# Seven products for every second row-block pair, and column-pair totals carried through the PSUM banks by ScalarE

## The reference, cut to what matters

```python
h2 = rmsnorm(x, norm2_g[l])                                   # x: 256 x 2048
x  = x + jnp.square(jax.nn.relu(h2 @ w_up[l])) @ w_down[l]    # w_up 2048 x 8192, w_down 8192 x 2048
```

## Time and profile before

| | us |
|---|---|
| median of 3 runs (2057.11 to 2057.16) | 2057.12 |
| the profiled execution | 2057.14 |
| its span, first to last instruction | 2055.3 |
| TensorE busy | 2038.4 (99%) |
| VectorE busy | 1520.6 (74%) |
| ScalarE busy | 1058.5 (51%) |
| pair stage of the second turn, 594.69 to 678.95 | 84.26 |
| up stage after it, 678.95 to 768.70 | 89.75 |

### The profile page before, as it was taken

The page is one execution under the profiler, slowest core; times in us unless marked ns, Lnnn a source line. Parts: engine busy times, 40 slices in busy tenths (PEclk is TensorE's granted clock), DMA queues, the critical chain, the costliest instruction groups (busy, mean ns, idle before and its releaser), DMA issues.

```text
span 2055.3 us, 26947 instructions
## 1 busy us (share of the span) xinstructions
PE 2038.4 (99%) x10644; PEld 1709.3 (83%) x10644; DVE 1520.6 (74%) x1961; ACT 1058.5 (51%) x1382; POOL 192.1 (9%) x196
## 2 busy tenths in 40 slices
PE   9999999999999999999999999999999999999999
PEld 7887788887887887888888877888788878878887
DVE  7767566788779769867677775666986896797674
ACT  6557644454455445444455586444544554554442
POOL 5253100000000000001023531000000000000000
PEclk9999999999999999999999999999999999999999
DMA  9477866666657665766665689566576566666663
GB/s 300 134 227 187 221 199 181 186 193 205 186 174 216 194 189 181 213 187 192 184 176 145 211 203 232 183 180 188 183 213 188 180 212 191 185 193 206 185 194 123
DMA packets 182879, 396.67 MB, mean 193 GB/s; under 512 B 13674, under 2 KB 22352, under 8 KB 182752
## 3 DMA queue, kind: packets, MB, share of 16 engines
q1 hardware_dynamic: 178064, 379.52, 61.1%
q0 software_dynamic: 4512, 15.33, 4.1%
q10 hardware_dynamic: 176, 0.09, 0.0%
HBM read 377.95 MB, written 2.12 MB: 185 GB/s over the span
## 4 chain that ended last, share of the span: by engine, by line
PE 85%; DVE 13%; issue 1%; DMA 1%; ACT 0%; SPq 0%; ACTq 0%
PE psum L570 23%; PE psum L594 23%; PE psum L597 12%; PE psum L574 12%; DVE w_lo L1086 4%; PE psum L641 4%; DVE t_lo L1094 2%; PE psum L604 2%; PE psum L644 2%; PE psum L608 2%; PE psum L605 2%; PE psum L697 1%; DVE x L1145 1%; PE psum L769 1%; DVE t_raw L1084 1%
## 5 line engine op out<-in xcount | busy, mean ns | idle before, releaser
L891 ACT CAST w_hi<-raw_ring 128x1024 fp32r<-128x1024 f32 (+1 forms) x720 | 747.4, 1042 | 857.0 <-PE psum L597 361.7
L1086 DVE TENSOR_TENSOR w_lo<-raw_ring,w_hi 128x1024 fp32r<-128x1024 f32 (+1 forms) x692 | 846.2, 1228 | 403.2 <-ACT w_hi L891 400.9
L594 PE MATMUL psum<-xt,w_hi 128*128 128x512 f32 x2048 | 515.1, 393 | 0.9 <-issue 0.3
L594 PEld LDWEIGHTS psum<-xt,w_hi 128*128 128x128 f32 x2048 | 368.4, 189 | 69.7 <-DVE x L1145 3.0
L597 PEld LDWEIGHTS psum<-xt,w_lo 128*128 128x128 f32 x2048 | 279.4, 190 | 20.0
L597 PE MATMUL psum<-xt,w_lo 128*128 128x256 f32 x2048 | 285.6, 282 | 0.0
L570 PE MATMUL psum<-w_hi,xt 128*128 128x512 f32 (+1 forms) x1152 | 281.4, 386 | 0.0
L570 PEld LDWEIGHTS psum<-w_hi,xt 128*128 128x128 f32 x1152 | 202.5, 189 | 40.3 <-issue 2.7
L570 PE MATMUL psum<-w_hi,ht_hi 128*128 128x512 f32 x512 | 203.1, 397 | 0.0
L570 PE MATMUL psum<-w_hi,ht_lo 128*128 128x512 f32 x512 | 199.8, 390 | 0.0
L641 PE MATMUL psum<-w_hi,ht_lo 128*128 128x512 f32 x384 | 149.5, 389 | 0.0
(11 more groups left out here) (200 smaller groups left out, 2140.8 us busy)
## 6 DMA issues: line engine op xcount, KB each, us to landing
raw_ring<-in_w_up_dram SPq DMA_DIRECT2D x256, 512.0 KB, 4.0
raw_ring<-in_w_down_dram SPq DMA_DIRECT2D x256, 512.0 KB, 4.2
raw_ring<-in_w_in_dram SPq DMA_DIRECT2D x128, 512.0 KB, 4.7
raw_ring<-in_w_out_dram SPq DMA_DIRECT2D x64, 512.0 KB, 4.9
w_lo<-raw_ring POOLq DMA_DIRECT2D x28, 512.0 KB, 6.9
raw_ring<-in_w_in_dram SPq DMA_DIRECT2D x16, 256.0 KB, 2.8
x<-in_x_dram SPq DMA_DIRECT2D x8, 256.0 KB, 7.8
out_dram<-x SPq DMA_DIRECT2D x3, 512.0 KB, 3.3
```

The lines of the kernel that those rows point to most:

```text
L594: pe.matmul(bank[:, f, :], w_hi[:, w, j, f * P:(f + 1) * P], both, start=kt == 0, stop=False, skip_group_check=True)
L891: act.copy(w_hi[:, u % AHEAD, :, 0:cols], raw_ring[:, u % RAWS, :, 0:cols]).then_inc(hi_ready, 1)
L1086: dve.tensor_tensor(w_lo[:, u % AHEAD, :, 0:cols], raw_ring[:, u % RAWS, :, 0:cols], w_hi[:, u % AHEAD, :, 0:cols].bitcast(F32), ALU.subtr ...
```

## The change

`SEVEN` becomes (1, 3, 5, 7) for both column pairs: each second pair of row blocks, and the last one of a column pair too. That is eight of sixteen in a turn. Column pair d = 1 now begins with plain units.

The totals of d = 0 no longer are added up in SBUF by VectorE. ScalarE copies them out of the banks at the border (`take_totals`), and at the start of the next turn of the layer copies them back into banks 0 to 3 (`give_totals`), where the products of that turn are added to them.

The last seven-product pair of a column pair is done in another order: second unit first, then the first, then all matmuls with `t_hi`, then the three with `t_lo`. The quarter adds follow it through `pair_done`. `last_unit` is gone. A seven-product pair reports its second unit as done before its `t` products, and its end through a semaphore of its own, `sevens_done`.

```diff
-SEVEN = ((2, 4, 6), (0, 2, 4, 6))
+SEVEN = (1, 3, 5, 7)
...
-            def seven_products(pl, s, d, kp, a, b, outs):
+            def seven_products(pl, s, d, kp, a, b):
...
+                new = first and (d == 1 or pl.i == 0)
...
                 if first and d == 0:
                     pe.wait_ge(evicted[0], pl.evictions(18))
+                    if pl.i:
+                        pe.wait_ge(totals_in, pl.l * (LOOPS - 1) + pl.i)
                 if first and d == 1:
-                    pe.wait_ge(pair_out, outs - PAIR_OUTS + 1)
+                    pe.wait_ge(totals_out, pl.l * LOOPS + pl.i + 1)
...
+                if last:
+                    quarters()
+                    own()
+                else:
+                    own()
+                    quarters()
...
                 if seven is not None and seven[0] == 1:
+                    if pair_at(pl, u)[1:] == (1, 2 * SEVEN[0] + 1):
+                        take_totals(pl, pair_at(pl, u)[0])
                     act.wait_ge(t_raw_ready, seven[1] + 1)
+                    if seven[1]:
+                        act.wait_ge(sevens_done, seven[1])
                     act.copy(t_hi[:, :, :], t_raw[:, :, :]).then_inc(t_hi_ready, 1)
...
+            def take_totals(pl, turn):
+
+                act.wait_ge(sevens_done, pl.l * SEVENS + (2 * turn + 1) * len(SEVEN))
+                act.copy(totals[:, :, :], psum[:, 0:4, :]).then_inc(totals_out, 1)
+
+            def give_totals(pl):
+
+                act.wait_ge(evicted[0], pl.evictions(18))
+                act.wait_ge(totals_out, pl.l * LOOPS + pl.i)
+                act.copy(psum[:, 0:4, :], totals[:, :, :]).then_inc(totals_in, 1)
...
             def mlp(pl, s, part, buf, c, k, n):
...
+                if part == "pair" and c == 0 and k == 0 and pl.i:
+                    give_totals(pl)
                 if pl.l < DEPTH - 1 or s + AHEAD < UNITS:
                     split_hi(pl, s + AHEAD)
...
-                if part == "pair" and c == 0 and k == 2 * KPS - 3:
-                    dve.wait_ge(unit_done, pl.unit(s + 1 + AHEAD))
-                    take_totals(pl)
                 if part == "pair" and k == 2 * KPS - 2:
-                    take_quarters(pl, s + 1, c)
+                    take_quarters(pl, s, c)
```

More of the change, by code:

```diff
@@ L645, in pair_steps @@
                     mm.then_inc(unit_done, 1)
[L647 to L653, removed]
-            def seven_products(pl, s, d, kp, a, b, outs):
-                i, first = SUMMED.index(kp), kp == SEVEN[d][0]
+            def seven_products(pl, s, d, kp, a, b):
+                i, first, last = SEVEN.index(kp), kp == SEVEN[0], kp == KPS - 1
                 _, number = seven_at(pl, s)
+                new = first and (d == 1 or pl.i == 0)
                 if d == 0:
@@ L671, in s_tile @@
                     return [t[:, i, n, :] for t in (s_hi, s_lo)]
[L673 to L680, removed]
@@ L681, in seven_products, with own @@
-                freed(2)
-                three(quarter(0, 1), s_tile(3), w_tile(s + 1, 1), kp == 0)
-                pe.wait_ge(t_lo_ready, number + 1)
[L684 to L687, removed]
+                def own():
+                    pe.wait_ge(hi_ready, pl.unit(s + 1))
+                    three(psum[:, 0, :], h_tile(a, 0), w_tile(s, 0), new, lambda: unit_is_split(pl, s))
+                    three(psum[:, 1, :], s_tile(0), w_tile(s, 1), new).then_inc(unit_done, 2 if last else 1)
@@ new lines, in quarters @@
+                def quarters():
+                    pe.wait_ge(hi_ready, pl.unit(s + 2))
+                    mm = three(quarter(0, 0), h_tile(b, 0), w_tile(s + 1, 0), False, lambda: unit_is_split(pl, s + 1))
+                    if last:
+                        mm.then_inc(pair_done, 1)
+                    mm = three(quarter(0, 1), s_tile(3), w_tile(s + 1, 1), False)
+                    mm.then_inc(pair_done if last else unit_done, 1)
+                if last:
+                    quarters()
[3 more added lines that the diff above has]
+                    quarters()
@@ new lines, in seven_products @@
+                products = [(quarter(1, 0), h_tile(b, 1), 2, False), (psum[:, 2, :], s_tile(1), 1, new), (psum[:, 3, :], s_tile(2), 0, new)]
+                pe.wait_ge(t_hi_ready, number + 1)
+                for bank, (a_hi, a_lo), t, start in products:
+                    pe.matmul(bank, a_hi, t_hi[:, t, :], start=start, stop=False, skip_group_check=True)
+                    pe.matmul(bank, a_lo, t_hi[:, t, :], start=False, stop=False, skip_group_check=True)
+                pe.wait_ge(t_lo_ready, number + 1)
@@ L689, in warm @@
+                for n, (bank, (a_hi, a_lo), t, start) in enumerate(products):
+                    mm = pe.matmul(bank, a_hi, t_lo[:, t, :], start=False, stop=True, skip_group_check=True)
+                    if last and n == 0:
+                        mm.then_inc(pair_done, 1)
+                mm.then_inc(sevens_done, 1)
             def warm(n):
@@ L1127, in quarter_x @@
                 return x[:, r, (2 * d + h) * CW:(2 * d + h + 1) * CW]
[L1129 to L1134, removed]
             def take_quarters(pl, s, d):
-                done = pl.at(2 * LOOPS * 3, 3 * d, 6)
                 for n, (r, h) in enumerate([(1, 1), (0, 0), (0, 1), (1, 0)]):
-                    if n < 3:
-                        dve.wait_ge(pair_done, done + n + 1)
+                    if n == 0:
+                        dve.wait_ge(unit_done, pl.unit(s + AHEAD))
                     else:
-                        dve.wait_ge(unit_done, pl.unit(s + 1 + AHEAD))
+                        dve.wait_ge(pair_done, pl.at(LOOPS * 6, 3 * d + n, 6))
                     v = quarter_x(r, h, d)
```

43 lines of the change are left out of this document (21 added, 22 removed).

## The result

| | before | after |
|---|---|---|
| median, us (5 runs each) | 2057.11 (2056.70 to 2057.16) | 2064.91 (2064.50 to 2065.15) |
| ratio after / before, 95% interval | | 1.004 (1.0029 to 1.0051) |
| profiled execution / its span, us | 2057.14 / 2055.3 | 2065.15 / 2063.3 |

The account below looks back on a forecast made before the run. VectorE's gapless queue was taken to bound each pair stage's first half. Two first turns at -0.55 and four later ones at +2.5 add 8.9 to 2057.14: 2066.0 us, own range 2062 to 2070, widened to 2058.5 to 2071 for 8 in 10.

Parts of the forecast that it names:

- VectorE's queue without the copies: Pair stage's start to first quarter add: changes of -2.20, +1.20, -0.60 and +0.25 sum to -1.35, adds at 42.0 us.
- The border and the stage: Between column pairs: TensorE starts 2.6 us after the adds begin, then 39.5 us; pair stage 84.1 against 84.28, -0.15.
- The up stage: At the up stage's start TensorE's 0.4 us wait goes: -0.4 us in each turn.
- The copy back: Second and third turns: ScalarE's 1.91 us copy into banks delays unit 4's cast; VectorE stands 3.04 us, arriving whole at the border.
- TensorE's waits inside the half: Later turns, first half: 2.2 us for banks at unit 2, probably 1 us at units 6 and 7, not added.
- The clock: A granted clock below 1.00 after the new waits was named a sign of being wrong; the trace showed 1.00 everywhere.
- The sum: Whole run: first turns -0.55 twice, -1.1; other four +2.5 each, +10.0; 2057.14 + 8.9 = 2066.0 us.
- TensorE the bound: Pair stages: VectorE's queue has unseen slack, stages -2.8 twice and -0.8 four times, 2048.3 us; chance 0.09, including the busy-time rule.
- Copy back free: Start of later turns: the copy into the banks costs VectorE nothing, all six turns gain 0.55, 2053.8 us; chance 0.04.
- made good: Before the border: half the delay recovered by waits counted as busy time, 6 us less, 2060.0 us; chance 0.07.
- came on top: TensorE's late units 6 and 7 add 1.1 us four times, with the copy at its upper price: 2071.9 us; chance 0.08.
- The rule of the Trainium skill: Optimize the highest-occupancy engine, TensorE: 18 fewer matmuls, 4.1 us off, 2053.0 us; shares the 0.09 chance of faster.

Follow-up runs that it names:

- the two kernels without the stall: Changed kernel with the copy back moved behind the cast of unit 4, 2054.44 us; changed kernel with no copy back, VectorE adding totals behind its quarter adds, 2053.24 us.
- The first experiment: Changed kernel with one swap on ScalarE: the copy of the totals into the banks stands behind the cast of unit 4; 2054.44 us.
- the third: Changed kernel with three extra small sums on VectorE per pair stage: ahead of the border 2082.39 us, behind it 2064.97 us.
- the last two kernels: Three quarter adds moved earlier, upon the kernels with early first t_hi and t_lo: 2042.60 us with copy back behind the cast, 2042.30 us with VectorE's totals.

## Why the prediction held, step by step

- **VectorE's queue without the copies.** 42.0 us from the stage's start to the quarter adds; measured 41.96 in both first turns, 41.97 in the two kernels without the stall. The 1.35 taken off is 1.35. The two kernels with three more sums show the premise at work: 2.20 us later ahead of the border, nothing behind it.
- **The border and the stage.** 84.1 was forecast, 84.07 and 84.08 measured. A wait of 1.4 us at the border remained, 0.8 in three of the later turns, where "1 us or more" was forecast. ScalarE's copy out started 42.3 us into a first turn and not at 41.3, and stayed hidden.
- **The up stage** lost 0.37 or 0.38 for 0.4 forecast (89.38). Its VectorE adds end at 681.54 for a start at 681.11.
- **The copy back.** Its duration was taken as 1.91 and is 1.87. It starts 5.64 us into the stage (5.66 forecast); VectorE stands 2.91 (3.04). Shown as the cause by the kernel that only changes the order of copy and cast: 10.5 us off between the profiled executions, four times 3.0 less the 1.5 of the slow stage. The later turns take 87.09 for 87.2.
- **TensorE's waits inside the half.** 2.14 for 2.2 at the banks. At units 6 and 7, 1 us was forecast and 0.64 came, in the one turn of four whose granted clock was 1.00; in the other three TensorE was later by its slow matmuls and did not wait. That they are not added to the sum held, since TensorE still waited at the border.
- **The clock.** The forecast set no price on a lower clock, since its trace had none, and it named a granted clock below 1.00 after the new waits as a sign of being wrong. That sign came, in three of the four later turns. It was a gap in the working, and that it did no harm to the number is luck: it cost nothing in this kernel because it fell into TensorE's slack. The first experiment (1.5 us once) and the third (1.2 to 1.4 us three times) show what it costs where there is none.
- **The sum.** 2066.0 forecast, 2064.9 measured. Of the 1.1 us, four times 0.1 is the shorter copy and stand, 0.5 is gone outside the stages of the forecast (the DMA wait above all, which has nothing to do with the change), 0.2 is the distance from the profiled execution to the median; the rest is roundings that go both ways.

Of the rivals, "TensorE the bound" would have given 2048.3 and fell with the border waits. Its figure for the path of a later turn was right, though: 81.7 and 2.2 us, which is what fills the later stages (84.08) once the stall is gone. "Copy back free" has nearly the result of the experiment that takes the stall away: 2053.8 worked out, 2054.4 measured. Nothing of the 3.0 us was made good, and nothing came on top.

The rule of the Trainium skill ("Perfetto Trace Analysis", identifying the most-contended engine) did not help here: by busy time TensorE leads with 99%, by its weight loading, one of the two measures which that page prefers for this engine, it still leads with 83% to VectorE's 74%, but the half stage was VectorE's, as its 43 us with hardly a gap told. Moving work out of those 43 us brought what the rule would have looked for on TensorE. Once that is done, in the last two kernels, TensorE is indeed the bound. The other one ("ScalarE: Activation LUTs", on writes to PSUM) can't be seen either way: the copy of 2048 columns into the banks took 1.87 us, the one out of them into SBUF 1.86, but the engine reads from the other memory in each.

## What to carry to other kernels

What a copy costs on an idle engine depends on its place in that engine's queue, not on the engine's share of busy time: ask what stands behind it and who takes that next. ScalarE was half idle, and the copy's effect on TensorE was hidden; its effect on the cast behind it was not, and one place further down the same copy cost 1.2 us in the whole run (2054.4 against 2053.2 with no copy back) in place of 11.7. Where a tight engine must do work anyway, put it behind the last thing that another engine waits for: VectorE's own 2.28 us there were free, where ScalarE's 1.87 us ahead of the cast cost 3.0. Free means free as long as there is slack: once the adds had moved up, the same 2.28 us delayed TensorE by 0.30. And look for the queue with no gap in the stretch that ends in the wait, since averages over the run show neither.

## What the hardware showed that was not expected

TensorE's clock fell behind waits of about 2 us, in some turns and not in others. The same wait of 2.14 us in the changed kernel, for the second and the third turn of the first layer (TensorE; the second turn's row is 601.79 above, behind which the clock was 1.00):

```profile
778.25 0.74 PE L609 MATMUL psum<-w_hi,ht_hi 128*128 128x512 f32 x1 [2.14 <-ACT psum L920]
778.79 0.63 PE L610 MATMUL psum<-w_hi,ht_lo 128*128 128x512 f32 x1
779.22 0.63 PE L613 MATMUL psum<-w_lo,ht_hi 128*128 128x512 f32 x1
779.65 0.63 PE L609 MATMUL psum<-w_hi,s_hi 128*128 128x512 f32 x1
```

Eight matmuls follow each other at 0.43 us in place of 0.227, some 1.6 us in all: the lower of its two levels, 1.2 GHz. It happened in three of four such turns of this kernel, in one of four with the copy behind the cast, in all four with the extra sums ahead of the border and in three of four with them behind it: 11 of 16. It also happened behind three of the six border waits of the kernel with the extra sums ahead of the border (1.82 to 1.84 us). No pair stage of any kernel here shows it behind a wait of 1.65 us or less. What decides between turns with the same wait was not found.

ScalarE moves 2048 fp32 columns from SBUF into PSUM in 1.87 us, as it does in the other direction (1.86), and within 0.05 us of the line through its casts of 1024 and 1536 columns (1.05 and 1.48, which gives 1.91).
